# Half of the sparse tokens' residual comes by SyncE in mid-stage, and GpSimd makes the sparse tokens' last sum

## What is computed

```python
h_res = h_res + merged @ w_out                    # the residual, h1 below
h2 = rms_norm(h_res, norm_peer_g)
e_idx, gate = top16_of_each_of_8_heads(h2 @ w_query, sub_keys)
a = gelu(einsum('cd,chkd->chk', h2, expert_u[e_idx]))
h_res = h_res + einsum('chk,chkd->cd', gate * a, expert_v[e_idx])
```

## Time and profile before

| | |
|---|---|
| median of 3 runs | 1953.23 us (1952.56 to 1955.71) |
| the profiled execution | 1951.24 us, of which the span of its instructions is 1949.3 us |
| TensorE busy in the span | 1940.0 us |
| VectorE busy | 1664.4 us |
| ScalarE busy | 1122.1 us |
| GpSimd busy | 664.4 us |
| granted TensorE clock | 1.00 |
| DMA over the span | 566.50 MB, 291 GB/s |
| DMA from 1400 us on (the V part) | 201.53 MB, 367 GB/s |

### The profile page before, as it was taken

How to read it: one execution, slowest core, us unless ns; L and a number is a source line. 1 busy time by engine, 2 the same in 40 slices (tenths; PEclk the granted TensorE clock), 3 DMA queues, 4 the chain that set the end, 5 groups by cost and what they waited for, 6 DMA issues and landing times.

```text
span 1949.3 us, 32645 instructions
## 1 busy us (share of the span) xinstructions
PE 1940.0 (100%) x11722; PEld 1765.4 (91%) x11722; DVE 1664.4 (85%) x2523; ACT 1122.1 (58%) x1589; POOL 664.4 (34%) x409
## 2 busy tenths in 40 slices
PE   9999999999999999999999999999999999999999
PEld 8899989998988888999999999999888888888887
DVE  8777778777888777999999999998888988888887
ACT  7565556555677455656665665655555455555555
POOL 0301110011000001887777877686222221333220
PEclk9999999999999999999999999999999999999999
DMA  6745654565455556999999999999999999999997
GB/s 246 252 160 194 204 191 159 188 204 194 162 173 192 185 173 228 336 341 341 334 334 341 345 326 355 336 384 356 358 364 387 381 374 371 381 376 381 371 379 270
DMA packets 137575, 566.50 MB, mean 291 GB/s; under 512 B 44008, under 2 KB 52080, under 8 KB 88112
## 3 DMA queue, kind: packets, MB, share of 16 engines
q1 hardware_dynamic: 87152, 414.05, 58.1%
q0 software_dynamic: 49936, 149.49, 22.9%
q10 hardware_dynamic: 432, 2.37, 0.3%
HBM read 548.31 MB, written 16.88 MB: 290 GB/s over the span
## 4 chain that ended last, share of the span: by engine, by line
PE 90%; DMA 4%; DVE 3%; ACT 1%; issue 1%; DVEq 0%; ACTq 0%; SPq 0%
PE psum L946 25%; PE psum L923 16%; PE psum L616 15%; PE psum L928 10%; PE psum L620 8%; PE psum L602 3%; PE psum L601 3%; PE psum L606 3%; DMA raw<-v_rows 2%; DMA arena<-u_cols 1%; ACT whi L479 1%; DVE xr L487 1%; DVE wlo L487 1%; PE psum L818 1%; PE psum L1000 0%
## 5 line engine op out<-in xcount | busy, mean ns | idle before, releaser
L473 DVE TENSOR_TENSOR wlo<-raw,whi 128x1024 fp32r<-128x1024 f32 x242 | 296.1, 1231 | 110.3 <-PE psum L620 72.2
L923 PE MATMUL psum<-xr,whi 128*128 128x384 f32 x2048 | 380.9, 337 | 0.0
L946 PE MATMUL psum<-whi,xr 128*128 128x512 f32 x1512 | 364.0, 390 | 0.3 <-DVE xr L1888 0.2
L923 PEld LDWEIGHTS psum<-xr,whi 128*128 128x128 f32 x2048 | 351.2, 188 | 0.5 <-ACT whi L479 0.2
L946 PEld LDWEIGHTS psum<-whi,xr 128*128 128x128 f32 x1512 | 283.6, 188 | 60.4 <-ACT whi L479 1.0
L479 ACT ACTIVATE whi<-raw 128x2048 fp32r<-128x2048 f32 x168 | 320.9, 1910 | 27.5 <-DMA raw<-v_rows 17.0
L616 PE MATMUL psum<-xr,whi 128*128 128x512 f32 x1296 | 330.2, 397 | 0.0
L466 ACT ACTIVATE whi<-raw 128x1024 fp32r<-128x1024 f32 x244 | 250.4, 1054 | 110.7 <-DMA raw<-stream 52.9
L1388 POOL DMA_INDIRECT arena<-v_rows,small x64 | 142.2, 2222 | 399.5 <-DVE arena L1852 396.0
L616 PEld LDWEIGHTS psum<-xr,whi 128*128 128x128 f32 x1296 | 232.6, 189 | 43.6 <-issue 0.2
L487 DVE TENSOR_TENSOR wlo<-raw,whi 128x1024 fp32r<-128x1024 f32 (+1 forms) x126 | 197.6, 1573 | 23.4 <-issue 19.9
(11 more groups left out here) (283 smaller groups left out, 3236.4 us busy)
## 6 DMA issues: line engine op xcount, KB each, us to landing
raw<-stream SPq DMA_DIRECT2D x244, 512.0 KB, 3.3
raw<-v_rows SPq DMA_DIRECT2D x85, 1024.0 KB
raw<-u_cols SPq DMA_DIRECT2D x84, 1024.0 KB
arena<-v_rows SPq DMA_DIRECT2D x43, 1024.0 KB, 7.9
arena<-u_cols SPq DMA_DIRECT2D x42, 1024.0 KB, 6.8
gates<-arena POOLq DMA_DIRECT2D x8, 1536.0 KB, 9.7
small<-gates SPq DMA_DIRECT2D x62, 192.0 KB, 8.2
arena<-x_t SPq DMA_DIRECT2D x4, 544.0 KB, 6.6
```

What stands on the lines that cost most here:

```text
L473: nc.vector.tensor_tensor(wlo[:, k % 2 * HALF:(k % 2 + 1) * HALF], raw[:, s * HALF:(s + 1) * HALF], f(whi[:, s * HALF:(s + 1) * HALF]), AL ...
L923: mm(bank(at, 0, 2 * TD), hi_w[:, c * P:(c + 1) * P], z_all[:, :, c, 0:TD // TS, :], start=c == 0, stop=False)
L946: last = mm(at[:, (b * 4 + j * 2 + n) * 512:(b * 4 + j * 2 + n + 1) * 512], weights, src, start=begin, stop=end, skip_group_check=True)
```

## The change

SyncE loads `h1_high` itself, in the V part behind the load that it issues at c = 40, and GpSimd no longer does. GpSimd, after it has issued the transfer of line 1437, waits for it to land and makes the sparse tokens' last sum; VectorE no longer does. The store of the sum (line 568) waits for the same semaphore as before, `sparse_out`.

```diff
@@ SyncE, in the loop over the blocks
                 if c == 1:
                     sp.wait_ge(row_used, ROWS)
                     sp.dma_start(acc[TS:P, :], h1_rows[TS:P, D:2 * D]).then_inc(acc_in, 16)
+                if c == 40:
+                    sp.dma_start(h1_high[0:TS, :], h1_rows[0:TS, D:2 * D]).then_inc(rows_back[1], 16)
                 if c % 2 == 0 and 0 <= c < B_V - 4:
                     sp.wait_ge(scaled, c + 2)
                     load_gates(c // 2 + 2)
@@ GpSimd, its end
             pool.wait_ge(row_used, 2 * ROWS)
             pool.dma_start(res[TS:P, :], acc[0:TS, :]).then_inc(acc_moved, 16)
-            pool.dma_start(h1_high[0:TS, :], h1_rows[0:TS, D:2 * D]).then_inc(rows_back[1], 16)
+            pool.wait_ge(acc_moved, 16)
+            nc.gpsimd.tensor_tensor(res[TS:P, :], res[TS:P, :], acc[TS:P, :], ALU.add).then_inc(sparse_out, 1)
@@ VectorE, the loop over the V blocks
                     V.tensor_tensor(rows_at, rows_at, h1_high[0:TS, half], ALU.add).then_inc(low_residual, 1)
-                if c == B_V - 6:
-                    dve.wait_ge(acc_moved, 16)
-                    V.tensor_tensor(res[TS:P, :], res[TS:P, :], acc[TS:P, :], ALU.add).then_inc(sparse_out, 1)
```

## The result

| | before | changed |
|---|---|---|
| median of 19 runs, us | 1953.41 (1948.31 to 1958.12) | 1957.82 (1953.40 to 1964.68) |
| ratio to before | 1 | 1.0023, 95% interval 1.0015 to 1.0030 |
| profiled execution: time, span | 1951.24, 1949.3 | 1957.82, 1955.8 |

0.0023 x 1953.4 is 4.5 us, 2.9 to 5.9 by the interval. The median lies 0.4 us above the top of the range that was given (1957.4). The profiled executions differ by 6.5 us in their spans.

What follows compares the result with a forecast made beforehand. TensorE was taken to bound the kernel: 1951.24 + 0.2 (load) + 1.3 (GpSimd's sum) - 0.1 (VectorE's sum removed) = 1952.6 us for the profiled execution. For a median, 1953.23 + 1.4 = 1954.6 us, range 1951.8 to 1957.4.

Steps and rivals of the forecast that it cites:

- The bound (TensorE, with VectorE's time worth nothing): Whole kernel: TensorE, busy 1940.0 of 1949.3 us, sets the time; removing VectorE's 2.29 us sum gains 0.1 us, at most 0.5.
- The load in mid-stage: At c = 40: the residual's load delays everything behind it by 1.36 us, costing 0.2 us, between 0 and 0.8.
- block 44: Mid-stage: block load behind the residual's; ScalarE done with it at 1562.16, TensorE begins at 1562.32, so it just fits.
- The upper bound: Mid-stage load: at most 0.8 us, from a block 2.10 us late at 1451 that cost TensorE 0.75 us.
- the train of late blocks: Rival, mid-stage: the full queue makes several blocks each cost 0.75 us; with three 2.3 us, 1956.8 with the tail; chance 0.08.
- GpSimd's sum: Tail: the added sum of 2048 columns takes 5.5 us, extrapolated from sums of 144 and 256 columns.
- What it does to VectorE: Tail: GpSimd's sum shuts out VectorE's two-SBUF-input sums for its whole length; TensorE stalls 1.3 us waiting for low parts.
- The rivals for the tail: Tail: VectorE not held up, 1953.0, chance 0.25; GpSimd in earlier, 1956.5, chance 0.07; GpSimd late, 1957.5 or more, chance 0.08.
- the rival of the late start: Tail: GpSimd idles 6.56 us again before its sum, costing 4.1 us at least; 1957.5 or more; chance 0.08.
- The range: Whole kernel: 1951.8 to 1957.4 us, likely cases 1953.0 to 1956.8 widened by the runs' spread, 0.7 below and 2.5 above.

Runs made afterwards that it cites:

- load_only: Kernel before with only the load of the low rows' residual moved to SyncE at c = 40, sum still on VectorE: 1956.54 us, ratio 1.0015.
- double_sum: Kernel before with the last sparse sum moved to GpSimd and made twice, first into a place nobody reads: 1960.79 us, ratio 1.0038.
- pieces_sum: Changed kernel with its residual load in 16 pieces behind the gates from c = 40 to 55: 1954.26 us, ratio 1.0002.
- sum_only: Kernel before with only the last sparse sum moved to GpSimd, its load staying at the end: 1953.69 us, ratio 0.9996; run once more, 1.0014.
- load_behind_gates: As load_only, but at c = 40 the load stands behind the gates instead of ahead: 1955.48 us, ratio 1.0011.
- two_extra_64: Kernel before plus two unread transfers at c = 40, ahead of the gates, each to 64 partitions x 8 KB: 1965.64 us, ratio 1.0065.
- two_extra_128: Kernel before plus two unread transfers at c = 40, ahead of the gates, each to 128 partitions x 4 KB: 1958.01 us, ratio 1.0018.
- after_again: The changed kernel, unaltered, timed again beside the kernel before: 1958.84 us, ratio 1.0032.

## Why the prediction was wrong, step by step

- **The bound (TensorE, with VectorE's time worth nothing).** Right. Taking 2.29 us off VectorE gained nothing that any kernel shows.
- **The load in mid-stage: 0.2 us, at most 0.8.** This is the step that failed. It is 2.9 us by load_only's ratio, and 5.3 us in the profiled execution. Three terms of it were wrong. The transfer's length was taken as 0.52 MB / 385 GB/s = 1.36 us from a row about transfers to 128 partitions; to 64 partitions it is, by the estimate above, about twice that, and one such transfer cost what two to 128 did (2.9 and 3.5 us). The working followed block 44 only, with a margin of 0.16 us, and not the gates, which were named as standing behind the load and were what VectorE, and behind it TensorE, in fact waited for. And what a stall does to the clock was put at nothing: it fell to 0.50 and cost 1.7 of the 5.3 us. The upper bound, one block that came 2.10 us late, was an event of another size, not an end of the range. A rival called the train of late blocks had nearly the right time (1956.8) at a chance of 0.08, for a reason that was half right: the queue had no room, but it was one long stall and not several blocks of 0.75 us.
- **GpSimd's sum: 5.5 us.** It is 4.6 to 4.7 us (double_sum, pieces_sum); 5.03 in the changed kernel holds 0.5 us in which VectorE's running sum was still ahead. The extrapolation over seven times the columns was too steep; the Trainium skill's 4497 ns, which the prediction set beside it, was nearer.
- **What it does to VectorE, 1.3 us in the tail.** The mechanism was right: the start at 5.96 us behind the issue, VectorE shut out for the length of the sum (its product stretched to 4.78 us), and TensorE waiting for the low parts behind it. The size was near, 1.0 us in the profiled execution, but by luck: what came through VectorE's low parts was 0.5 us where 1.3 had been worked out, since the sum was shorter, and the other half came another way. It spreads more than foreseen (1.0 to 3.2 in five traces with one sum, the largest with a late block among its causes), since its start hangs on a transfer that takes some 6 or 9.9 us. The other 0.6 us came through the load of `h1_low`, which stands behind the last block's load in SyncE's order; the prediction followed the block and not the load behind it.
- **The rivals for the tail.** GpSimd started neither early nor late by an idle start of its own, and VectorE was held up. But in three traces the sum did start some 4 us late, through the transfer of 9.9 us; the tail then lost 2.5 to 3.2 us, where the rival of the late start had 4.1.
- **The range.** It took the spread of three runs (0.7 us below their median, 2.5 above). The 19 runs of the kernel before spread by 5.1 and 4.7 us. What single late blocks cost TensorE differs between executions as well: in sum_only, two groups elsewhere in the stage came 5.57 and 5.32 us after the one before (at 1632.87 and 1851.51), and the kernel before had one of 5.41 us too (at 1681.12), which the prediction did not look at.

## What to carry over

A queue that runs full has no room for one more large item: work out how long it is held up at the rate of that item's own shape, then follow every transfer behind it, the small ones too, to the engine that waits for it in order. Half a megabyte in sixteen pieces passed unnoticed where one piece of it cost 3 us. An engine with slack is no free place for work if its instruction shuts out those of a busy one: the price is the length of that instruction less the lead that the bound engine has at that point. And where the bound engine is TensorE, look at its granted clock behind every stall: the stall may cost more than the wait.

## What the runs showed of the hardware

- With a transfer to 64 partitions in the queue, the windows of 5 us quoted here moved 190 to 318 GB/s at a DMA share of 0.99 to 1.03; with transfers to 128 alone they moved 385 to 426. The share tells that the engines are occupied, not that they move data at full rate; it is to be read beside the GB/s.
- The cost of a full queue is not proportional: one transfer to 64 partitions cost 2.9 us, two some 12.7.
- Behind waits of TensorE of 3.39 us (the changed kernel), 2.49 (load_behind_gates), 6.51 (two_extra_64), 4.10 (double_sum) and 2.00 us (load_only) the granted clock stood at 0.50 in the matmuls that followed, which cost 1.5 to 1.9 us each time; in two_extra_128, behind 3.22 us, it cost 2.9. Behind the waits of 1.79 us (sum_only) and 1.68 us (after_again) it stayed at 1.00.
- A GpSimd sum of 64 x 2048 in float32 takes 4.6 to 4.7 us (5.0 to 6.0 where an instruction of VectorE was ahead of it), and a VectorE sum with two SBUF inputs that meets it is held until it ends (0.35 us became 4.67 to 4.78, in every trace where they met).
- The transfer of 0.52 MB within SBUF took 5.5 to 6.2 us in 11 traces and 9.9 us in 3, with nothing between; what decides is open.
